# Attention gates with their weights stationary in four column groups, and the empty bank jobs moved to POOL

## The chip, the cores and the metric

The kernel runs on one core of one Trainium2 chip. The metric is the device time of one execution in microseconds, the median of several runs. All data are f32.

## The reference

Two transformer blocks in a row, over 256 tokens of 1024 channels, batch 1.

- The first block modulates the input by a projection of `c` (`ada_w`), projects it by `w_in`, and runs two branches: a gated linear recurrence over 8 heads (HGRN2: q, f, v, g) and a sparse attention over 8 heads (NSA: q, compressed, selected and window keys and values). Both are merged under gates, projected (`w_out`), and followed by a mixture of 32 experts with two chosen per token.
- The second block has cross attention on `mem`, a convolution, a bidirectional RWKV recurrence and 16 experts that choose their tokens.

What the change touches is one line of the attention:

```
gate = sigmoid(h @ w_in[:, 6656:6680] + b_in[6656:6680])     # 24 = 8 heads x 3 kinds
o = gate[..., 0:1] * o_c + gate[..., 1:2] * o_s + gate[..., 2:3] * o_w
```

`h` is 256 tokens x 1024 channels, so the product has only 24 columns.

## The kernel before

Each engine has its own instruction stream, written out in order; they meet only at semaphores.

**Weights.** SP loads weight tiles of up to 128 x 4096 f32 (2 MB) into a ring of 6 slots, in the order of the list `w`. Tile n is issued once the last job that reads tile n - 6 is full (`tile_read`, `last_job`). Biases go to a small area of rows (`brow`). POOL issues the small loads and the scattered ones.

**Banks.** The output memory of TensorE has 8 banks of 128 x 512. Every group of products is a job with a number that `PLAN1` and `PLAN2` give in order; job j uses bank j mod 8. `start(j)` makes TensorE wait until job j - 8, the one before in the bank, has been copied out. `fills` raises the bank's "full" semaphore, `frees` its "free" one; `is_full` and `is_out` wait for them. So two counters for each bank replace a list of dependencies, and a job that isn't needed must still raise both. The plan has 6 such empty jobs, `unused`, between the attention and the branch products `br`. TensorE raises all twelve counts itself, just ahead of `br`.

**Products.** `mm` is one product, recorded at L1447 for nearly all of them. An f32 product shows in the trace as two matmul records and two weight loads. `hT` is the modulated input, channels on partitions, 8 chunks (k) of 128 channels x 256 tokens. `chunk_pair` gives outputs with channels on partitions: a 128x128 piece of weights is stationary, 256 tokens move. `token_half` gives outputs with tokens on partitions: 128 tokens of `hT` are stationary, the weights' columns move. Where 4 products with 32 stationary columns each are given to the four column groups (`32 * q:32 * q + 32`), they run side by side and leave four partial sums, which a product with a selection matrix such as `fold` adds up (`modulation`, the compression's `part` and `hid`).

**The order around the change, on TensorE.** q, f, v, g, nq, kvc, ks, vs, kw, vw; then the gates: for each of two token halves a bias row and 8 products of 24 moving columns (`token_half`, L1447); then `part` (2 jobs of 32 products, from the compression's weights `cw1`), `hid` (their folding), `kcmp`, `vcmp`; then the recurrence (KT, att, and per head updates, outputs and half of a merge gate), `turn_heads` 0 to 2, and the attention by heads: `scores(0)`, and for each head h `scores(h + 1)`, modulation products (`ada2`) and `weigh(h)`. For h = 0 `turn_heads(3)`, which waits for the last two normalised heads of DVE, comes before the products of merge gate 2.

**On ScalarE (ACT).** It copies out most jobs, in the same order. Around the gates: `ks`, `kw`; L1035 Sigmoid of the gates; L1040 the two `part` copies; L1043 Silu of `hid`; L1046 and L1048 `kcmp`, `vcmp`. A function of another table set needs an ACT_TABLE_LOAD just ahead of it: Exp at L1031, then Sigmoid, then Silu.

**On POOL.** It waits for `rel` to be copied out, writes the rows of relative biases to DRAM (`relrow`, 2 MB), waits for that, and then for the values `v` and `vs`, and for the gates to be full (their bias row lies where it writes), and masks the values for the recurrence.

Of the kernel before, what the change touches and what calls it, by code (L numbers as in the profile page):

```python
# [53 lines left out]
def constants():  # L54
    t = np.arange(P)
    same = (t[:, None] // CHUNK) == (t[None, :] // CHUNK)
    return pack({
        "ident": np.eye(P),
        "upto": same & (t[:, None] <= t[None, :]),
        "scan": np.tile((np.arange(T) % CHUNK != 0), (P, 1)),  # L60
        "seen": (t[:, None] + P * np.arange(TT)[None, :]) >= 31,
        "odd": t[:, None] // CHUNK % 2 == np.arange(2)[None, :],
        "mhalf": np.full((P, 1), -0.5),
        "eps_conv": np.full((P, 1), 1e-5),
        "eps_group": np.full((P, 1), 64e-5),
        "fold": (t[:, None] % 32 == np.arange(30)[None, :]),
        "gkey": np.tile(4 - np.arange(4), (P, 1)),
        "ekey": np.tile(NE1 - np.arange(NE1), (P, 1)),
        "pick": (t[:, None] % CHUNK == np.arange(CHUNK)[None, :]),
        "fold16": (np.where(t // 32 % 2 == 0, t % 32, t % 32 - 16)[:, None] == np.arange(16)[None, :]),  # L70
        "until": t[:, None] <= t[None, :],
        "fold36": (np.where(t < 64, t, t - 92)[:, None] == np.arange(36)[None, :]),
    })
# [19 lines left out]
def scan_masks():  # L93
# [5 lines left out]
    for d, late in enumerate((i < j, i > j)):  # L99
        parts[f"strictT{d}"] = late  # L100
        parts[f"uptoT{d}"] = late | (i == j)
        for m in MERGES:
# [4 lines left out]
CST, CST_A = constants()  # L107
MSK, MSK_A = scan_masks()
UP0 = 4
PAGED = (4, 5, 12, 13)  # L110

VA = dict(b=0, mg=52, l0=68, l1=76, hgn=84, nmix=92, nmem=100, nffn=108)
# [1 line left out]
VROWS = (116, 62, 93, 64)  # L114
N_VEC = 23

PLAN1 = [("mod", 1), ("hT", 2), ("modc", 1), ("q", 4), ("hTb", 2), ("modb", 1), ("modcb", 1), ("rel", 3), ("f", 4), ("v", 4), ("g", 4), ("nq", 4),
         ("kvc", 2), ("ks", 1), ("vs", 2), ("kw", 1), ("vw", 2), ("gate", 1), ("part", 2), ("hid", 2), ("kcmp", 1), ("vcmp", 1),
         ("KT", 4), ("att", 4), ("hg", 3 * HEADS + 4), ("OHT", 3),
         ("nsa", 6 * HEADS + 15), ("unused", 6), ("br", 8),  # L120
         ("g1b", 2), ("y", 4), ("memT", 4), ("h2T", 4), ("modc2", 1), ("vm", 1),
         ("logitT", 1), ("route", 1), ("gain", 1), ("km", 1), ("rank1", 1), ("general", 19)]
IN2 = (2, 3, 4, 0, 1)
# [10 lines left out]
def build(nc, A, out):  # L134
    with ExitStack() as ctx:
# [141 lines left out]
        def last_job(n):  # L277

            name, i = w[n][0], [m for m in range(N2) if w[m][0] == w[n][0]].index(n)
            if name == "mg":  # L280
                return jM0(3) if i == 0 else jG(2 * i + 1)
            if name == "ada":
                return J(("mod", "modb")[i // 2]) if i < 4 else jA(i - 4)
            if name == "in2":
                return (J("in2", 1), J("in2", 3), J("in2", 5), J("qa"), J("in2b", 1))[i]
            if name in ("gate", "cw1"):
                return J({"gate": "gate", "cw1": "part"}[name], i)
            if name in ("q", "f", "v", "g", "nq", "kvc", "br", "wout2"):
                return J({"wout2": "y2"}.get(name, name), 2 * i + 1)
            if name == "wout":  # L290
                return J("y", 2 + i)
            return J(*{"kvs": ("vs", 1), "kvw": ("vw", 1), "cw2": ("vcmp", 0), "mem": ("km", 0), "router": ("logitT", 0),
                       "up2": ("a1", 1), "router2": ("scoreT", 0)}[name])
# [28 lines left out]
        VV = v4(vv[:], TT, 2)  # L322
        blocks = [arena(7)[:, 0:962], arena(7)[:, 1024:1986]]
        hpart = v3(arena(9)[:, 384:640], 2)
        h1 = v3(arena(9)[:, 0:60], 2)
        kcmp = arena(9)[:, 64:94]
        vcmp = v3(arena(9)[0:NBLK, 128:384], 2)
# [75 lines left out]
        for h in range(HEADS):  # L403
            if h + 1 < HEADS:
                nsa += [("scores", h + 1, i) for i in range(3)]
            if h == 0:
                nsa += [("turn", 3, 0), ("gate", 2, 0)]
            nsa += [("ada", i, 0) for i in ADA_BEFORE[h]]
            nsa += [("out", h, i) for i in range(2)]
            if 0 < h < HEADS - 2:  # L410
                nsa.append(("gate", h + 2, 0))
            nsa += [("ada", i, 0) for i in ADA_WITHIN[h]]
            nsa.append(("out", h, 2))
# [334 lines left out]
        def _(pool):  # L748
# [48 lines left out]
            load(relrow, relsb.unsqueeze(1).to_broadcast([HEADS, P, 2 * T]), "rel_stored")  # L797
            pool.wait_ge(S("rel_stored"), 16)

            def bias_rows(dst, h0, count, name):  # L800

                for t in range(TT):
                    src = bass.AP(relrow.tensor, 255 - P * t + P * 2 * T * h0,
                                  [[2 * T - 1, P], [P * 2 * T, count], [1, T]])
                    load(dst[:, :, t * T:t * T + T], src, name)
# [157 lines left out]
        def _(act):  # L963
# [67 lines left out]
            nc.scalar.activation(L[:], B[:], ACT.Exp).then_inc(S("forget_out"), 1)  # L1031
            chunks("ks", 0, ks, ACT.Identity, 44)
            chunks("kw", 0, kw, ACT.Identity, 48)
            is_full(act, J("gate"))
            frees(nc.scalar.activation(gates, v3(bank(J("gate"), 48), TT), ACT.Sigmoid), J("gate"))  # L1035
            for i in range(2):
                is_full(act, J("part", i))
                if i == 0:
                    is_full(act, J("part", 1))
                frees(nc.scalar.copy(hpart[:, i, :], bank(J("part", i), P)), J("part", i))  # L1040
            for i in range(2):
                is_full(act, J("hid", i))
                frees(nc.scalar.activation(h1[:, i, :], bank(J("hid", i), 30), ACT.Silu, bias=col(1, VB["b1k"] + i)),  # L1043
# [68 lines left out]
            exps(0)  # L1112
            for h in range(HEADS):
                if h == 0:
                    heads_turned(3)
                    gate_pair(2)
                carry_turned(h)
                if h + 1 < HEADS:
                    exps(h + 1)
# [296 lines left out]
        def _(pe):  # L1416
# [164 lines left out]
            for name in ("v", "g"):  # L1581
                for i in range(2):
                    n = tile(name)
                    for t in range(TT):
                        ins, j = token_half(name, 2 * i + t, slot(n, (8, 512)), 0, 512, hT, t)
                        fills(ins, j)
            for i in range(2):
                n = tile("nq")
                for c in range(2):
# [4 lines left out]
            for s in "sw":  # L1594
                n = tile("kv" + s)
                chunk_pair("k" + s, 0, slot(n, (8, 512)), 0, hT)
                for t in range(TT):
                    ins, j = token_half("v" + s, t, slot(n, (8, 512)), 256, 256, hT, t)
                    fills(ins, j)
            n = tile("gate")  # L1600
            j = job("gate")
            for t in range(TT):
                ins, _ = token_half("gate", 0, slot(n, (8, 24)), 0, 24, hT, t, brow_at(n)[1][:, 0:24],
                                    bank(j)[:, 24 * t:24 * t + 24], j)
            fills(ins, j)

            for i in range(2):
# [4 lines left out]
                for p in range(32):  # L1612
                    q = p % 4
                    ins = mm(bank(j, P)[32 * q:32 * q + 32, :], blocks[i][:, 30 * p:30 * p + 32],
                             slot(n, (32, 128))[:, p, :], p < 4, p >= 28)
                fills(ins, j)
            for i in range(2):
                is_out(pe, J("part", i))
                j = job("hid", i)
# [152 lines left out]
            for h in range(HEADS):  # L1772
# [1 line left out]
                    scores(h + 1)  # L1774

                if h == 0:
                    turn_heads(3)
                    n_mg.append(tile("mg"))
                    products(start(jG(2)), slot(n_mg[0], (8, 512)), 0, hT)
                for i in ADA_BEFORE[h]:  # L1780
                    pe.wait_ge(S("slide_ready"), 2)
                    ada2(i)
# [2 lines left out]
            for j in range(4):  # L1785
                is_out(pe, jOHT(j))
            is_out(pe, jT(HEADS - 1, 2))
            for i in range(6):
                j = job("unused", i)
                pe.sem_inc(full[j % BANKS], 1)  # L1790
                pe.sem_inc(free[j % BANKS], 1)  # L1791
            for i in range(4):
                n = tile("br")
                for c in range(2):
# [1644 lines left out]
```

## Time and profile before

| | us |
|---|---|
| median of 3 runs | 1648.62 |
| lowest and highest | 1647.56, 1656.34 |
| the profiled execution, its own time | 1652.61 |
| its span (first to last instruction) | 1650.4 |
| PE busy | 1346.3 (82%) |
| DVE busy | 425.1 (26%) |
| ACT busy | 278.7 (17%) |
| POOL busy | 124.7 (8%) |

PE is TensorE, PEld its weight loads, which run beside the products. The granted clock is a share of 2.4 GHz: 1.00 is 2.4 GHz and 0.50 is 1.2 GHz. Its mean over the span is 0.901. A DMA share of 1 means that all 16 DMA engines are busy. The times in the views are counted from the start of the span.

### The profile page before, as it was taken

How to read it: one execution, taken by the hardware profiler on the slowest of the kernel's cores; microseconds unless marked ns; L12 is line 12 of the kernel's file. 1: busy time of each engine (PE TensorE's matmuls, PEld its weight loads, DVE VectorE, ACT ScalarE, POOL GpSimd, SP SyncE). 2: the span in 40 equal slices, each digit the busy share in tenths (PEclk: the TensorE clock that was granted, in tenths of full speed). 3: DMA queues.
4: the chain of work that ended last, by engine and by line, in shares of the span. 5: the costliest groups of instructions: out<-in, count | busy, mean ns of one | idle time of the engine just before them, and what ended most of it. 6: DMA issues, size and time to landing. Idle time of an engine off the chain costs nothing.

```text
span 1650.4 us, 27106 instructions
## 1 busy us (share of the span) xinstructions
PE 1346.3 (82%) x11720; PEld 757.5 (46%) x11720; DVE 425.1 (26%) x910; ACT 278.7 (17%) x626; POOL 124.7 (8%) x283
## 2 busy tenths in 40 slices
PE   5999999999999877777777689877887576766675
PEld 4756887777663332322322278676432122212221
DVE  1012147430273222222222234563520000000001
ACT  0201224550011111110111113332110100100000
POOL 4000013000000000000000004021000000000000
PEclk9999999999999998988998989987888778787778
DMA  9865383566469999999999690300989999999996
GB/s 347 266 175 210 106 296 120 186 222 207 156 261 425 426 428 427 429 428 428 428 429 427 285 340 29 95 4 8 414 326 428 428 429 428 428 428 428 428 427 272
DMA packets 86997, 513.90 MB, mean 311 GB/s; under 512 B 9033, under 2 KB 13562, under 8 KB 62338
## 3 DMA queue, kind: packets, MB, share of 16 engines
q1 hardware_dynamic: 82306, 502.84, 75.1%
q0 software_dynamic: 3936, 9.19, 2.3%
q8 instruction: 66, 1.08, 0.3%
q10 hardware_dynamic: 672, 0.65, 0.2%
q14 instruction: 17, 0.14, 0.0%
HBM read 507.77 MB, written 3.15 MB: 310 GB/s over the span
## 4 chain that ended last, share of the span: by engine, by line
PE 50%; DMA 41%; DVE 4%; issue 2%; ACT 1%; SPq 1%; POOL 0%; DVEq 0%; PEldq 0%; ACTq 0%
PE ps L1447 41%; DMA ring<-in_exp_w 19%; DMA arena<-in_w_e_down 19%; PE ps L2241 4%; DMA ring<-in_w_e_up 2%; PE ps L1536 2%; DMA ring<-in_w_in 1%; DVE stats L2600 1%; PE ps L2013 1%; DMA arena<-in_mem 1%; PE ps L2441 0%; PE ps L1491 0%; PE ps L1676 0%; SPq L636 0%; PE ps L1672 0%
## 5 line engine op out<-in xcount | busy, mean ns | idle before, releaser
L1447 PE MATMUL ps<-ring,arena 128*32 128x512 f32 (+4 forms) x1844 | 264.4, 646 | 105.5 <-DMA ring<-in_exp_w 89.1
L1447 PE MATMUL ps<-ring,hTs 128*32 128x512 f32 (+3 forms) x1056 | 232.4, 624 | 33.9 <-DMA ring<-in_w_e_up 21.3
L1447 PE MATMUL ps<-hTs,ring 128*128 128x256 f32 (+2 forms) x992 | 216.3, 385 | 0.1
L1447 PEld LDWEIGHTS ps<-ring,arena 128*32 128x32 f32 (+1 forms) x1844 | 84.8, 128 | 265.1 <-issue 241.5
L1447 PEld LDWEIGHTS ps<-hTs,ring 128*128 128x128 f32 (+2 forms) x992 | 183.6, 189 | 29.0 <-issue 4.2
L1447 PE MATMUL ps<-arena,vv 128*32 128x512 f32 (+2 forms) x560 | 98.2, 756 | 86.3 <-DMA arena<-in_w_e_down 81.9
L1447 PEld LDWEIGHTS ps<-ring,hTs 128*32 128x32 f32 (+1 forms) x1056 | 88.1, 141 | 152.2 <-issue 114.1
L1447 PEld LDWEIGHTS ps<-arena,vv 128*32 128x32 f32 (+2 forms) x560 | 28.8, 148 | 139.4 <-DMA arena<-in_w_e_down 88.5
L1447 PE MATMUL ps<-arena,hTs 128*32 128x512 f32 x480 | 92.5, 621 | 0.0
L3001 DVE COPY hTs<-ps 64x512 f32<-64x512 f32 x32 | 22.2, 693 | 259.7 <-PE ps L1447 259.7
L1177 ACT COPY arena<-ps 128x512 f32<-128x512 f32 x32 | 18.7, 585 | 388.4 <-PE ps L1991 388.4
L1447 PE MATMUL ps<-arena,ring 128*128 128x256 f32 (+2 forms) x320 | 71.2, 388 | 3.8 <-PEq L1791 2.6
L1447 PEld LDWEIGHTS ps<-arena,ring 128*128 128x128 f32 (+1 forms) x320 | 60.0, 193 | 14.8 <-issue 6.7
L2013 PE MATMUL ps<-arena 64*128 64x512 f32 x256 | 63.0, 610 | 1.6 <-DVE arena L3010 1.6
L3381 DVE TENSOR_TENSOR vv<-vv,ps 64x512 f32<-64x512 f32 x16 | 11.0, 690 | 204.7 <-ACT vv L1396 204.7
L3375 DVE TENSOR_TENSOR hTs<-ps,nffn 128x128 f32<-128x128 f32 x32 | 7.8, 286 | 204.5 <-PE ps L1447 204.5
L857 POOL COPY arena<-arena 128x128 f32 (+1 forms) x64 | 16.9, 293 | 437.9 <-PE ps L1991 417.3
L1447 PEld LDWEIGHTS ps<-cst,low 64*128 64x128 f32 (+1 forms) x544 | 33.1, 189 | 27.4 <-issue 27.4
L1396 ACT ACTIVATE vv<-ps 64x512 f32<-64x512 f32 x16 | 9.4, 590 | 201.1 <-PE ps L1447 201.1
L1447 PE MATMUL ps<-arena 128*32 128x512 f32 (+6 forms) x264 | 43.3, 411 | 0.0
L2529 PE MATMUL ps<-hTs,vv 64*128 64x512 f32 x128 | 38.2, 724 | 1.4 <-ACT hTs L1402 1.4
L1402 ACT COPY hTs<-ps 128x512 f32<-128x512 f32 x16 | 9.4, 585 | 172.9 <-PE ps L1447 172.9
(464 smaller groups left out, 1432.2 us busy)
## 6 DMA issues: line engine op xcount, KB each, us to landing
ring<-in_exp_w SPq DMA_DIRECT2D x92, 2048.0 KB, 22.2
arena<-in_w_e_down SPq DMA_DIRECT2D x28, 2048.0 KB, 25.6
ring<-in_w_e_gate SPq DMA_DIRECT2D x24, 2048.0 KB, 30.9
ring<-in_w_e_up SPq DMA_DIRECT2D x24, 2048.0 KB, 36.3
ring<-in_w_in SPq DMA_DIRECT2D x22, 2048.0 KB, 19.5
ring<-in_ada_w SPq DMA_DIRECT2D x12, 2048.0 KB, 17.2
arena<-in_w_e_up SPq DMA_DIRECT2D x8, 2048.0 KB, 34.6
arena<-in_w_e_gate SPq DMA_DIRECT2D x8, 2048.0 KB, 32.7
```

Source lines behind the costliest of these rows:

```text
L857: ins = nc.gpsimd.tensor_copy(gateR[:, t], mid(gatep1[:, t, cols], 4))
L1177: nc.scalar.copy(HT1, ps[:, m * 512:m * 512 + 512]).then_inc(S("hidT1_ready"), 1)
L1396: nc.scalar.activation(hid2, u[0:64], ACT.Silu).then_inc(S("silu2_ready"), 1)
L1402: nc.scalar.copy(YE, ps[:, 1024:1536]).then_inc(S("ye_ready"), 1)
L1447: return nc.tensor.matmul(o, lhsT, rhs, start=start, stop=stop)
L1536: ins = nc.tensor.matmul(o, wt[:, k, c * P:(c + 1) * P], hT[:, k, :], start=k == 0 and c % 2 == 0, stop=k == KC - 1, skip_group_check=True)
L2013: ins = nc.tensor.matmul(ps[:, b * 512:b * 512 + 512], HT1[r, 256 + t * P:256 + (t + 1) * P], YE1[r, :], start=False, stop=True, skip_grou ...
L2241: return nc.tensor.matmul(o, lhsT, rhs, start=start, stop=True, skip_group_check=True)
L2529: ins = nc.tensor.matmul(ps[:, b * 512:b * 512 + 512], HT2[r, 256 + t * P:256 + (t + 1) * P], YE[r, :], start=False, stop=True, skip_group ...
L2600: ins = nc.vector.bn_stats(bns[:, t, c, :], src[:, t, c * 512:(c + 1) * 512])
L3001: cp(part1, u[64:128]).then_inc(S("part_ready"), 1)
L3381: tt(hid2, hid2, ps[64:128, (e % 2) * 512:(e % 2) * 512 + 512], ALU.mult).then_inc(S("hid2_ready"), 1)
```

## The change

The gates are computed with the weights stationary. A chunk of 128 channels has 24 columns of gate weights; 32 are taken, so that a chunk brings some of its neighbour's. Chunk k goes to column group k mod 4, and 256 tokens move, 8 products in all, in a new job `gateT`. ACT copies its 128 x 256 result to the arena, and after `part` TensorE adds the four groups by a product of that copy with the selection matrix `fold24`, together with the bias row, in the job `gate`. ACT's Sigmoid now comes after the two `part` copies. The slot of the gates' weights is given back with `gateT`.

The empty jobs are 5 in place of 6, come before `nq`, and are raised by POOL after `relrow` is written, each once the job before it in its bank is out. For head 0, `turn_heads(3)` and the products of merge gate 2 change places, on TensorE, in the plan and on ACT.

```diff
+        "fold24": np.where(t < 96, t % 32, t - 104)[:, None] == np.arange(24)[None, :],
+UNUSED = 5
-... ("g", 4), ("nq", 4),
-         ("kvc", 2), ("ks", 1), ("vs", 2), ("kw", 1), ("vw", 2), ("gate", 1), ("part", 2), ("hid", 2), ...
+... ("g", 4), ("unused", UNUSED), ("nq", 4),
+         ("kvc", 2), ("ks", 1), ("vs", 2), ("kw", 1), ("vw", 2), ("gateT", 1), ("part", 2), ("gate", 1), ("hid", 2), ...
-         ("nsa", 6 * HEADS + 15), ("unused", 6), ("br", 8),
+         ("nsa", 6 * HEADS + 15), ("br", 8),
+        gateT = arena(9)[:, 640:896]
-                nsa += [("turn", 3, 0), ("gate", 2, 0)]
+                nsa += [("gate", 2, 0), ("turn", 3, 0)]
 # POOL, after relrow is stored
+            for i in range(UNUSED):
+                j = J("unused", i)
+                pool.wait_ge(free[j % BANKS], j // BANKS)
+                pool.sem_inc(full[j % BANKS], 1)
+                pool.sem_inc(free[j % BANKS], 1)
 # ACT
-            is_full(act, J("gate"))
-            frees(nc.scalar.activation(gates, v3(bank(J("gate"), 48), TT), ACT.Sigmoid), J("gate"))
+            is_full(act, J("gateT"))
+            act.wait_ge(S("blocks_ready"), 2)
+            frees(nc.scalar.copy(gateT, bank(J("gateT"), T)), J("gateT"))
             for i in range(2):
                 ... # the two part copies
+            is_full(act, J("gate"))
+            frees(nc.scalar.activation(gates, v3(bank(J("gate"), 48), TT), ACT.Sigmoid), J("gate"))
...
+                    gate_pair(2)
                     heads_turned(3)
-                    gate_pair(2)
 # TensorE
+            turn[0] += UNUSED
-            n = tile("gate")
-            j = job("gate")
-            for t in range(TT):
-                ins, _ = token_half("gate", 0, slot(n, (8, 24)), 0, 24, hT, t, brow_at(n)[1][:, 0:24],
-                                    bank(j)[:, 24 * t:24 * t + 24], j)
+            n_gate = tile("gate")
+            j = job("gateT")
+            flat = slot(n_gate, (8, 24)).rearrange("p k n -> p (k n)")
+            for k in range(KC):
+                q = k % 4
+                o = 24 * k - 8 * (q // 3)
+                ins = mm(bank(j, T)[32 * q:32 * q + 32, :], flat[:, o:o + 32], hT[:, k, :], k < 4, k > 3)
             fills(ins, j)
             ... # the two part jobs
+            is_out(pe, J("gateT"))
+            j = job("gate")
+            for t in range(TT):
+                o = bank(j)[:, 24 * t:24 * t + 24]
+                mm(o, ones_row, brow_at(n_gate)[1][:, 0:24], True, False)
+                ins = mm(o, gateT[:, t * P:(t + 1) * P], C("fold24"), False, True)
+            fills(ins, j)
...
-                    turn_heads(3)
                     n_mg.append(tile("mg"))
                     products(start(jG(2)), slot(n_mg[0], (8, 512)), 0, hT)
+                    turn_heads(3)
...
-            for i in range(6):
-                j = job("unused", i)
-                pe.sem_inc(full[j % BANKS], 1)
-                pe.sem_inc(free[j % BANKS], 1)
```

## Rows read from the trace of the kernel before

**Rows 1.** The page, DMA rate in 40 equal slices of the span.

```profile
GB/s 347 266 175 210 106 296 120 186 222 207 156 261 425 426 428 427 429 428 428 428 429 427 285 340 29 95 4 8 414 326 428 428 429 428 428 428 428 428 427 272
```

**Rows 2.** Busy time by stage: length, PE, PEld, DVE, ACT, POOL, clock, DMA share, GB/s.

```profile
67.00:219.00 152.00, 151.94 (x578) 109.36 (x576) 26.06 (x38) 22.76 (x38) 1.10 (x1) 1.00 0.59 177
...
376.00:436.00 60.00, 57.50 (x258) 50.16 (x259) 7.17 (x11) 0.30 (x1) 1.61 (x3) 0.97 0.50 167
436.00:498.00 62.00, 60.33 (x294) 34.42 (x292) 38.84 (x88) 8.98 (x20) 4.75 (x9) 1.00 0.63 242
548.00:934.00 386.00, 296.90 (x2242) 113.66 (x2240) 94.32 (x158) 41.88 (x78) 19.38 (x79) 0.90 1.01 427
```

**Rows 3.** The chain that ended last: start, us, what.

```profile
189.82 40.72 PE ps L1447 x300
...
231.57 1.18 issue
...
437.43 9.57 DMA arena<-in_mem
```

**Rows 4.** Timeline at the gates: start, us, engine, line, operation, count, idle before.

```profile
225.11 5.38 PE L1447 MATMUL ps<-ring,arena 128*32 128x128 f32 x128
...
225.22 0.21 ACT L1035 ACTIVATE stats<-ps 128x48 f32<-128x48 f32 x1 [10.77 <-PE ps L1447]
...
231.07 1.28 ACT L1043 ACT_TABLE_LOAD   x1
232.37 0.46 ACT L1043 ACTIVATE arena<-ps,low 128x30 f32<-128x30 f32 x2
```

**Rows 5.** Busy time and granted clock in pieces of the gates' stretch.

```profile
219.10:219.43 0.33, 0.33 (x3) 0.29 (x2) 0.21 (x1) 0.00 (x0) 0.00 (x0) 1.00 0.00 0
219.43:221.40 1.97, 1.97 (x18) 1.93 (x17) 0.21 (x1) 0.00 (x0) 0.00 (x0) 1.00 0.53 108
221.65:225.10 3.45, 3.45 (x17) 3.40 (x16) 0.00 (x0) 0.00 (x0) 0.00 (x0) 0.52 1.05 404
225.10:228.30 3.20, 3.20 (x61) 2.96 (x64) 0.00 (x0) 0.21 (x1) 2.85 (x5) 0.50 0.94 281
228.70:230.50 1.80, 1.79 (x68) 1.52 (x56) 0.00 (x0) 0.00 (x0) 0.00 (x0) 1.00 1.03 397
```

**Rows 6.** Products in four column groups: a chain row (256 columns), a timeline row.

```profile
1040.90 10.57 PE ps L1447 x192
...
371.44 1.90 PE L1447 MATMUL ps<-ring,low 128*32 128x512 f32 x16
```

**Rows 7.** Timeline, 275 to 301 us: scores, heads, gate product, DVE's softmax.

```profile
275.10 3.68 PE L1447 MATMUL ps<-arena 128*128 128x15 f32 x24
...
280.58 0.66 PE L1696 MATMUL ps<-cst,arena 128*128 128x128 f32 x4 [1.80 <-DVE arena L2775]
...
281.08 7.07 PE L1447 MATMUL ps<-hTs,ring 128*128 128x256 f32 x32
...
299.44 1.28 DVE L2821 TENSOR_SCALAR arena<-arena,stats 128x15 f32<-128x15 f32 x6
```

**Rows 8.** Timeline and granted clock at the empty jobs.

```profile
375.93 0.37 ACT L1110 COPY arena<-ps 128x256 f32<-128x256 f32 x1 [5.46 <-PE ps L1447]
...
378.50 1.77 PE L1447 MATMUL ps<-arena,ring 128*128 128x256 f32 x4 [2.60 <-PEq L1791]
...
379.00:382.00 3.00, 3.00 (x8) 2.37 (x8) 0.00 (x0) 0.00 (x0) 0.00 (x0) 0.50 1.05 386
```

**Rows 9.** Evictions of `v` and `g`, and the write of `relrow`.

```profile
68.46 1.10 POOL L750 DMA_DIRECT2D relrow<-arena  x1 [40.30 <-ACT arena L1014]
...
102.18 0.69 DVE L2702 TENSOR_TENSOR arena<-ps,low 128x512 f32<-128x512 f32 x1 [3.32 <-PE ps L1447]
...
150.15 0.69 DVE L2702 TENSOR_TENSOR arena<-ps,low 128x512 f32<-128x512 f32 x1 [5.67 <-PE ps L1447]
...
relrow<-arena POOLq DMA_DIRECT2D x1, 2048.0 KB, 44.8
```

More of the change, by code:

```diff
@@ L115 @@
 N_VEC = 23
-PLAN1 = [("mod", 1), ("hT", 2), ("modc", 1), ("q", 4), ("hTb", 2), ("modb", 1), ("modcb", 1), ("rel", 3), ("f", 4), ("v", 4), ("g", 4), ("nq", 4),
-         ("kvc", 2), ("ks", 1), ("vs", 2), ("kw", 1), ("vw", 2), ("gate", 1), ("part", 2), ("hid", 2), ("kcmp", 1), ("vcmp", 1),
+PLAN1 = [("mod", 1), ("hT", 2), ("modc", 1), ("q", 4), ("hTb", 2), ("modb", 1), ("modcb", 1), ("rel", 3), ("f", 4), ("v", 4), ("g", 4), ("unused", UNUSED), ("nq", 4),
+         ("kvc", 2), ("ks", 1), ("vs", 2), ("kw", 1), ("vw", 2), ("gateT", 1), ("part", 2), ("gate", 1), ("hid", 2), ("kcmp", 1), ("vcmp", 1),
          ("KT", 4), ("att", 4), ("hg", 3 * HEADS + 4), ("OHT", 3),
-         ("nsa", 6 * HEADS + 15), ("unused", 6), ("br", 8),
+         ("nsa", 6 * HEADS + 15), ("br", 8),
          ("g1b", 2), ("y", 4), ("memT", 4), ("h2T", 4), ("modc2", 1), ("vm", 1),
@@ L286, in last_job @@
             if name in ("gate", "cw1"):
-                return J({"gate": "gate", "cw1": "part"}[name], i)
+                return J({"gate": "gateT", "cw1": "part"}[name], i)
             if name in ("q", "f", "v", "g", "nq", "kvc", "br", "wout2"):
```

## The prediction

> **What bounds the kernel now.** I began with the page's DMA slices: the rate lies at 4 to 350 GB/s in some of them and at 425 or more in the others [rows 1], so no one resource bounds the whole. The busy time by stage says which does where [rows 2]: from 67 to 219 us PE is busy 151.94 of 152.00 us; from 548 to 934 us the DMA share is 1.01 and PE is busy only 296.90 of 386. The edits lie in the first, PE-bound third. There, every microsecond in which PE works or waits is a microsecond of the span, if it also moves the start of the expert stream. It should: at 436 to 498 us the DMA share is 0.63 and in the 60 us before 0.50 [rows 2], so the stream is not yet full, and what its issues and the load of `mem` wait for are products and norms behind PE. The chain of waits agrees [rows 3]: an unbroken run of L1447 up to 230.5 us, an "issue" of 1.18 us that ends at 232.75, and much later the `mem` load at 437.43, which starts behind PE's last branch products. The gates, PE's wait for the normalised heads and its empty jobs all lie ahead of that load.
>
> **A. The gates (219.11 to 232.75 us).** Now: 16 products of 128x24 and two bias rows, 219.11 to 225.11, 6.00 us; then 128 records of the partial sums, 5.38 us; then ACT's two copies, a table load of 1.28 us, Silu, and PE goes on at 232.75 [rows 4]. Two records are one f32 product. The clock matters: it was 1.00 for the first eight gate products (1.97 us), then 0.52 for the second eight (3.45 us), 0.50 for the first part of the partial sums, and 1.00 again from 228.70, where 68 records took 1.80 us, 26 ns each [rows 5]. It fell from 2.4 to 1.2 GHz after 2.4 us of very narrow products.
>
> The new gateT product is 16 records of 128*32 stationary and 256 moving columns, in four column groups. The trace has the form: 192 such records took 10.57 us at clock 1.00, so 16 take 0.88; 16 records of twice the columns took 1.90, half of which is 0.95 [rows 6]. The outer bounds are 0.88 and, if the groups did not overlap, 16 x 0.22 us as in the full-width rows (32 records in 7.07 us, [rows 7]), 3.5 us. I take 0.96, the nearest rows. The partial sums then run behind wide products at full clock: 128 x 26 to 27.5 ns = 3.5 us (at worst 5.38 again). The fold job: two bias rows at 0.32 us (219.11 to 219.43) and two folds at 0.25 (1.97/8) = 1.14 us.
>
> On the new clock of this stretch: gateT ends at 220.07, the partial sums at 223.6, the fold at 224.75, and the `hid` products behind it at 225.4. ACT copies gateT (0.37 us, the 128x256 copy of [rows 8]) while PE is in the partial sums, so PE's new wait for it costs nothing; if that copy were late, the fold, `hid` and all of PE's queue would stand behind it. But the Sigmoid now stands between the copies and the Silu. Its table load of 1.28 us lay in time in which ACT had nothing to do (10.77 us idle before the Sigmoid, [rows 4]); now copies end at 224.1, Sigmoid's load at 225.4, Sigmoid (0.21) at 225.6, Silu's load at 226.9, and with 0.35 us from Silu's start to PE's, PE goes on at 227.3. Against 232.75 that is 5.4 us less. The moved load costs 1.5 us of what would be 6.9.
>
> From 223.6 to about 228.2 PE then has only narrow products (24, 30, 15 columns) and 1.9 us of nothing. In this trace 2.4 us of such work was followed by half clock, so I expect one fall here. Its price, from the fall of [rows 8]: 3.0 us at 0.50 and, as an estimate from it, 0.4 at its edges, half of which is lost, 1.7 us. Bounds: 0 and two such stretches, 3.4. A yields 3.7 us (2.0 to 5.4; with groups that do not overlap or slow partial sums down to 0).
>
> By the Trainium skill, ScalarE: Activation LUTs, "What ACT_TABLE_LOAD costs", a switch costs 1283 ns of load and about 1380 ns of drain. The load's length is that of the trace; the drain isn't seen (Silu starts 0.02 us after the load's end). With a drain counted as well for the moved load, A would be 2.3 instead of 3.7.
>
> **B. Gate product ahead of the last head turn (278.8 to 288.1 us).** PE ends the scores of head 1 at 278.78, waits 1.80 us for the normalised heads (DVE L2775), turns them in 0.66 and then does the 7.07 us gate product, whose inputs are long there [rows 7]. In the new order it runs in the gap: 278.8 to 285.9, then the turn, about 286.4 instead of 288.1. All 1.80 us are gained, since the modulation products that follow wait only for a DVE step ahead of those heads in its queue. What is late next: DVE's additions of masks to head rows that a load brings, and behind them the softmax of head 1, whose exps run on ACT behind the copies of head 0's turned weights and so move with PE; that DVE step ends at 300.72 [rows 7], 8 us after the additions have to be done. ACT's two evictions are swapped likewise; nothing waits on the turn before 376 us. Bounds 0 and 1.8.
>
> **C. The empty jobs.** PE stands idle 375.9 to 378.5, 2.60 us, for ACT's last copy (375.93 and 0.37 us) and then for its own twelve increments (its sequencer's L1791 is named as releaser) [rows 8]. Without them PE starts its products at about 376.6: 1.9 us. Behind this gap the clock is 0.50 from 379 to 382 [rows 8]; with a gap of 0.7 us I expect no fall, another 1.7 us (0 to 1.7, since the fall may not come in every execution). Together 3.6.
>
> By the Trainium skill, TensorE: Matmul & The Clock Gate, "A second HAM failure mode: psum-queue depth-cycling", frequent micro-idles between groups of products bring the clock down and up again. The trace agrees at 378.5 us; by that rule the new narrow stretch in A falls too, as counted, and a remaining 0.7 us gap in C could still do it, which would take C to 1.9.
>
> **D. Where the empty jobs go.** They now stand between `g` and `nq` and give banks a shift of 5 there. `nq` 0 to 2 wait for `g` 1 to 3 in place of `v` 0 to 2: the eight evictions of `v` and `g` run from 102.18 to 150.15, 6.9 us apart [rows 9], so each is over at least 6 us before its `nq` job, the first of which starts at 150. `nq` 3 comes at 150 + 3 x 6.9 = 170.7 and waits for POOL's first raise. POOL raises when the 2 MB write of `relrow` has landed (68.46 + 44.8 = 113.3) and, for the last, when `g` 0 is out (102.18 + 4 x 6.9 + 0.7 = 130.5) [rows 9]: 57 us of slack, nothing is paid, and what is queued behind the raises on POOL waits for the gates anyway. From the gates on all jobs keep their mutual distance. The 24 new constant columns are 12 KB, 0.04 us at the first slice's 347 GB/s. The tile loads released by gateT start 5 us earlier into a DMA whose share before 219 us is 0.59; nothing needs them before the modulation products of B. All this at 0; the bound is 0.3.
>
> **Sum.** 3.7 + 1.8 + 3.6 = 9.1 us. On the profiled execution: 1652.61 - 9.1 = 1643.5 (its span 1650.4 to 1641.3, with 2.2 us around it). The median of the runs is 1648.62, 4 us below it, so I forecast 1639.5.
>
> **The rivals.**
> 1. The clock stays up in A's narrow stretch (the trace shows no fall behind the partial sums, where `hid` and the products behind it were narrow too): 10.8 us, 1637.8.
> 2. The gates give less: half clock also over the partial sums (+1.9) or groups that don't overlap (+2.5), or two low stretches behind them (+1.7): 4.5 to 6.5 us gained, about 1643. For it: the partial sums ran at 0.50 in this trace. Against: what preceded them were 24-column products, which are gone.
> 3. Swallowed: the expert stream is DMA-bound and starts no earlier, 1648.6. For: DMA 1.01 from 548 us on. Against: 0.50 and 0.63 before, with issues that wait for PE. It would show as a longer DMA wait near 548 us. Smaller variants (other falls of the clock in later stages) give or take 2 to 4 us and end here too.
> 4. Slower: POOL raises too late. If `relrow` landed after 170.7 us instead of 113.3, PE would stand at `nq` 3, microsecond for microsecond; from 170.7 + 9.1 = 179.8 on the kernel is slower than before, at 190 us by 10 us: 1659. Only a write 66 us longer than the 44.8 seen would do it.
> 5. The change doesn't do what it says: DVE's heads come later than the gate product's end, or Sigmoid's load is put elsewhere. The second would help by 1.5 us.
>
> **Chances.** Forecast (1637.5 to 1641.5) 0.48; rival 1 0.12; rival 2 0.18; rival 3 0.16; rival 4 and anything slower 0.05; rival 5 0.01. The range reaches from rival 1 with 3 us below it to rival 3: 1634 to 1648. Half a per cent, about what a measurement of this kernel can tell from no change, is 8.2 us, or 1640.4. My forecast is just past it: faster by more 0.50 (two thirds of the forecast's share, rival 1, and some of rivals 2 and 5), within 0.45, slower 0.05.
>
> **What would show it.** Gates: one run of about 16 records in under 1.1 us at 219 us, partial sums in 3.5 us at clock 1.00, two table loads back to back before Silu, PE going on 8.2 us after the gates began. Heads: no wait for DVE L2775. Empty jobs: PE idle under 1 us before the branch products and 1.00 behind it. The `mem` load near 428 us. It is wrong if that load starts early and the end doesn't move, if the partial sums stay at 5 us, or if PE stands at `nq` 3.

## The result

The changed kernel takes 1639.33 us (median of 9 runs, 1636.01 to 1643.08). The kernel before, run beside it, takes 1650.31 us (9 runs, 1644.59 to 1656.83). The ratio is 0.9933, 95% interval 0.9914 to 0.9952. A later comparison (E11) gave 0.9954 [0.9939, 0.9969]. The forecast was 1639.5 us.

The profiled execution has a span of 1638.5 us, 11.9 less than the 1650.4 before. The chain of waits of the changed kernel (start, us, what), beside [rows 3]:

```profile
24.63 8.83 PE ps L1548 x32
...
189.79 34.32 PE ps L1459 x286
224.11 2.01 issue
226.12 0.92 PE ps L1459 x6
227.03 3.52 PE ps L1660 x16
...
369.64 84.75 PE ps L1459 x324
```

L1459 is what L1447 was. PE goes on at `kcmp` at 226.12 instead of 232.75, and its branch products start at 369.64 instead of 378.50 [rows 8]. The first row is a difference that isn't the change's: the same 32 records took 10.04 us in the trace of before. The clock was 0.50 from 24 to 30 us there and only from about 26 to 29 us here, and with a start 0.14 us earlier that gives 1.3 us.

The timeline of the changed kernel at the gates, which answers to [rows 4]:

```profile
217.77 1.07 PE L1459 MATMUL ps<-hTs,ring 128*32 128x256 f32 x16
...
218.66 3.68 PE L1459 MATMUL ps<-ring,arena 128*32 128x128 f32 x128
...
218.91 0.37 ACT L1045 COPY arena<-ps 128x256 f32<-128x256 f32 x1 [7.10 <-PE ps L1459]
...
222.46 0.43 ACT L1050 COPY arena<-ps 128x128 f32<-128x128 f32 x2 [3.17 <-PE ps L1459]
...
222.91 1.28 ACT L1052 ACT_TABLE_LOAD   x1
...
224.21 0.21 ACT L1052 ACTIVATE stats<-ps 128x48 f32<-128x48 f32 x1
224.43 1.28 ACT L1055 ACT_TABLE_LOAD   x1
225.73 0.46 ACT L1055 ACTIVATE arena<-ps,low 128x30 f32<-128x30 f32 x2
```

The gates' first product is 16 records that start 0.89 us before the partial sums; these run for 3.68 us, and two table loads with the Sigmoid between them stand ahead of Silu. The granted clock of the changed kernel there and behind it (length; busy PE, PEld, DVE, ACT, POOL; clock; DMA share; GB/s), beside [rows 5]:

```profile
219.00:222.00 3.00, 3.00 (x120) 3.00 (x114) 0.00 (x0) 0.29 (x1) 0.00 (x0) 1.00 0.95 309
223.00:226.00 3.00, 1.11 (x8) 0.96 (x8) 0.00 (x0) 2.96 (x5) 2.17 (x4) 1.00 1.05 394
227.00:230.00 3.00, 3.00 (x15) 3.00 (x15) 0.00 (x0) 1.83 (x6) 0.00 (x0) 0.50 1.05 385
230.50:233.00 2.50, 2.50 (x25) 2.50 (x24) 1.31 (x2) 0.65 (x2) 0.00 (x0) 1.00 1.01 373
```

The partial sums now run at 2.4 GHz. In the 3 us before 226 PE has 1.11 us of narrow products, and from 227 to 230 us, in the key turns, it is at 1.2 GHz: the fall that the forecast counted.

The swap and the gap ahead of the branch products in the timeline of the changed kernel, beside [rows 7, 8]; and the `mem` load, which started at 437.43 before:

```profile
270.09 3.68 PE L1459 MATMUL ps<-arena 128*128 128x15 f32 x24
273.61 7.07 PE L1459 MATMUL ps<-hTs,ring 128*128 128x256 f32 x32
280.52 0.60 PE L1718 MATMUL ps<-cst,arena 128*128 128x128 f32 x4
281.05 5.36 PE L1459 MATMUL ps<-ring,low 128*32 128x512 f32 x48
...
368.91 0.37 ACT L1122 COPY arena<-ps 128x256 f32<-128x256 f32 x1 [5.46 <-PE ps L1459]
...
369.64 1.53 PE L1459 MATMUL ps<-arena,ring 128*128 128x256 f32 x6 [0.77 <-ACT arena L1122]
...
426.88 0.71 POOL L753 DMA_DIRECT2D arena<-in_mem  x1 [48.18 <-DVE arena L2886]
```

No row of the first four has an idle time before it any more: the gate product starts 3.52 us after the scores, where the head turn started 5.48 us after them. The idle time ahead of the branch products is 0.77 us, released by ACT's last copy and not by PE's sequencer, and the clock stays at 1.00 behind it:

```profile
369.60:373.00 3.40, 3.36 (x16) 3.00 (x17) 0.00 (x0) 0.00 (x0) 0.00 (x0) 1.00 1.05 386
```

**Where the 11.9 us are, stage by stage in these two executions.** 1.3 us before 67 us, by the clock; 3.7 between the gates' start and the recurrence's first output (23.89 to 20.22); 2.0 at the swap; 1.8 in the gap ahead of the branch products and 1.7 in the 59 us behind it; 1.3 after the `mem` load. The stage from 66 to 219 us, into which the empty jobs went, is the same to 0.01 us.

### The profile page after: what moved, and what is told of

Same layout as the page of the kernel before. It is cut to its first block, busy times and chain, and to the rows that moved or that the text cites. A ratio compares the mean times of both kernels' runs of the same rounds, so it can differ in the third digit from the quotient of the medians.

```text
span 1638.5 us, 27083 instructions
## 1 busy us (share of the span) xinstructions
PE 1335.9 (82%) x11708; PEld 750.6 (46%) x11708; DVE 425.1 (26%) x910; ACT 279.5 (17%) x627; POOL 125.5 (8%) x283
## 4 chain that ended last, share of the span: by engine, by line
PE 52%; DMA 41%; DVE 3%; issue 2%; ACT 1%; SPq 1%; POOL 0%; DVEq 0%; ACTq 0%
PE ps L1459 42%; DMA arena<-in_w_e_down 19%; DMA ring<-in_exp_w 19%; PE ps L2259 4%; DMA ring<-in_w_e_up 2%; PE ps L1548 2%; DMA ring<-in_w_in 1%; PE ps L2031 1%; PE ps L1698 0%; SPq L639 0%; PE ps L1694 0%; DVE stats L2618 0%; PE ps L1503 0%; PE ps L2271 0%; PE ps L1759 0%
## 5 line engine op out<-in xcount | busy, mean ns | idle before, releaser
L1459 PE MATMUL ps<-ring,arena 128*32 128x512 f32 (+4 forms) x1844 | 263.9, 643 | 103.1 <-DMA ring<-in_exp_w 87.4
L1459 PE MATMUL ps<-ring,hTs 128*32 128x512 f32 (+2 forms) x1024 | 229.2, 641 | 42.1 <-DMA ring<-in_w_e_up 23.8
L1459 PE MATMUL ps<-hTs,ring 128*128 128x256 f32 (+2 forms) x1008 | 216.8, 384 | 0.1
L1459 PEld LDWEIGHTS ps<-ring,arena 128*32 128x32 f32 (+1 forms) x1844 | 83.6, 127 | 263.9 <-issue 241.7
L1459 PEld LDWEIGHTS ps<-hTs,ring 128*128 128x128 f32 (+2 forms) x1008 | 183.8, 188 | 29.4 <-issue 4.3
L1459 PE MATMUL ps<-arena,vv 128*32 128x512 f32 (+2 forms) x560 | 93.8, 722 | 85.3 <-DMA arena<-in_w_e_down 80.9
L1459 PEld LDWEIGHTS ps<-ring,hTs 128*32 128x32 f32 (+1 forms) x1024 | 82.9, 139 | 161.8 <-issue 115.3
L1459 PE MATMUL ps<-arena,hTs 128*32 128x512 f32 x480 | 93.9, 627 | 0.0
L1459 PEld LDWEIGHTS ps<-arena,vv 128*32 128x32 f32 (+2 forms) x560 | 28.3, 144 | 136.5 <-DMA arena<-in_w_e_down 87.4
L1459 PE MATMUL ps<-arena,ring 128*128 128x256 f32 (+2 forms) x320 | 69.5, 381 | 2.8 <-issue 2.0
L1459 PEld LDWEIGHTS ps<-arena,ring 128*128 128x128 f32 (+1 forms) x320 | 58.8, 190 | 13.3 <-issue 5.7
L1459 PEld LDWEIGHTS ps<-cst,low 64*128 64x128 f32 (+1 forms) x544 | 33.1, 189 | 27.4 <-issue 27.4
L1459 PE MATMUL ps<-arena 128*32 128x512 f32 (+6 forms) x264 | 43.3, 411 | 0.0
```

Of the source, the lines that this page charges most:

```text
L1459: return nc.tensor.matmul(o, lhsT, rhs, start=start, stop=stop)
```

## The experiments

Because the forecast came out so near, the question was whether its terms are right or only their sum. Each kernel's runs scatter by some 3 us (standard deviation), as much as a term is worth, so each experiment is read in two ways: by its timed ratio, and by the lengths of the stretches in its trace, which the later stages don't disturb. The table has the stretches that the change touches, from start times in the timelines, in us: from the gates' first product to `kcmp` (gates), on to the recurrence's first output (then), the two together (sum), from its last output group to the turn of head 0's weights (swap), from ACT's last copy to the branch products (gap), on to the `mem` load (branch), and from that load to the end (rest).

```
kernel                gates   then   sum    swap    gap   branch   rest     ratio [95%]
before                13.64  10.25  23.89   20.41   2.57   58.93  1212.97
E4  before again      13.67  11.81  25.48   20.41   2.54   58.70  1208.63
E2  empty jobs alone  10.40  10.25  20.65   20.40   0.74   57.24  1212.08   0.9993 [0.9972, 1.0014]
E3  swap alone        10.40  10.28  20.68   18.38   2.57   57.23  1212.89   0.9991 [0.9967, 1.0015]
E9  swap and empty    10.40  10.25  20.65   18.38   0.73   57.24  1217.25   0.9986 [0.9972, 1.0000]
E8  14 empty jobs     12.07  11.81  23.88   20.41   5.01   59.16  1209.41   1.0010 [0.9993, 1.0027]
E1  gates alone        8.34  12.74  21.08   20.41   2.27   58.92  1212.67   0.9998 [0.9978, 1.0019]
E10 gates and empty    8.34  11.87  20.21   20.40   0.73   57.24  1208.16   0.9955 [0.9940, 0.9970]
changed                8.35  11.87  20.22   18.38   0.73   57.24  1211.62   0.9933 [0.9914, 0.9952]
E11 changed again      8.34  12.71  21.05   18.39   0.73   57.24  1217.08   0.9954 [0.9939, 0.9969]
E7  one column group  10.92  12.77  23.69   18.38   0.73   57.24  1213.67   0.9963 [0.9945, 0.9981]
E5  fold late          6.81  11.82  18.63   18.39   0.73   57.23  1216.11   0.9935 [0.9913, 0.9957]
E6  key turns early    8.57   8.56  17.13   18.38   0.73   57.24  1213.31   0.9929 [0.9905, 0.9954]
E12 the same again     8.58   8.55  17.13   18.38   0.73   57.24  1209.06   0.9927 [0.9909, 0.9945]
```

**E1, the gates' part alone.** The changed kernel with the swap undone and its 5 empty jobs back on TensorE.

> The kernel before with the gates' part of the change alone (column groups, fold, Sigmoid behind the part copies; 5 empty jobs stay on TensorE ahead of the branch products, head turn stays first). Theory (three separate gains, gates 3.7, swap 1.8 to 2.0, empty jobs 3.5): 3 to 4 us faster, from the gates' start to the product after Silu 8.3 us in place of 13.6, one fall of the clock behind it, idle before DVE's heads 1.8 us and 2.2 us before the branch products as before. Rival (the gain of the whole is mostly luck with the clock in other places): this kernel within 1 us of before.

Measured: the gates' stretch is 8.34 us, as forecast, and the half clock behind it came and cost 2.5 us (12.74 for the 10.25 of the traces in which no fall came there). The timed ratio, 0.9998, shows nothing, with an interval that reaches to 3.6 us faster. By the trace the theory's path is right, but the whole stretch, 21.08 us, is then only 2.8 us shorter than in the first trace of before. By the time neither the theory nor the rival is decided.

**E2, the empty jobs alone.** The 6 empty jobs stand ahead of `nq` and POOL raises them.

```diff
-         ("nsa", 6 * HEADS + 15), ("unused", 6), ("br", 8),
+... ("g", 4), ("unused", 6), ("nq", 4), ...        # raised by POOL after relrow is stored
```

> The kernel before with the 6 empty jobs ahead of nq, raised by POOL, and nothing else changed. Theory: PE idle before the branch products 0.7 us in place of 2.6, granted clock 1.00 behind it in place of 0.50 for 3 us: 3.5 us faster (1.9 if before's clock does not fall in most executions). Rival: the fall at that place comes from something else than the gap and stays: 1.9 us or less. Second rival: POOL's raises make PE wait at the fourth nq job: a gap near 170 us; I expect none.

Measured: gap 0.74 us, and 57.24 us behind it, the length without a fall; no wait at the fourth `nq` job. By time it is 1.2 us faster with an interval from 4.6 faster to 2.3 slower, which decides nothing. The surprise was elsewhere. This kernel has the old gates, and in its timeline the second eight gate products take as long as the first, at full clock (timeline, then clock):

```profile
218.89 1.97 PE L1453 MATMUL ps<-ring,hTs 128*128 128x24 f32 x16
...
221.11 1.97 PE L1453 MATMUL ps<-ring,hTs 128*128 128x24 f32 x16
223.01 3.70 PE L1453 MATMUL ps<-ring,arena 128*32 128x128 f32 x128
```

```profile
218.50:220.50 2.00, 2.00 (x18) 1.90 (x17) 0.42 (x1) 0.00 (x0) 0.00 (x0) 1.00 0.34 62
220.50:222.20 1.70, 1.70 (x16) 1.63 (x15) 0.00 (x0) 0.00 (x0) 0.00 (x0) 1.00 0.97 354
```

The fall of the clock that [rows 5] show for the same instructions did not come: 4.4 us of 24-column products passed at 2.4 GHz.

**E3, the swap alone.**

> The kernel before with the products of merge gate 2 ahead of the last head turn and nothing else changed. Theory: the 1.80 us wait for DVE's heads is gone and no other wait takes its place: 1.8 to 2.0 us from the scores' end to the modulation products. Rival: the softmax of head 1 becomes the next wait and takes it back: PE idle over 0.3 us before its turned weights.

Measured: the stretch is 2.03 us shorter (18.38 for 20.41), the same in all eight traces with the swap but for 0.01 us, and 82.57 us follow it, up to ACT's last copy, in place of 82.56: nothing there takes it back. Of the 0.2 us above the wait of 1.80 [rows 7], 0.16 are the end of the scores: their last record ends 3.68 us after the first starts, and the gate product starts beside it, at 3.52. By time the kernel is 1.5 us faster, from 5.4 faster to 2.5 slower. The gap ahead of the branch products is there (2.57), but this time no fall behind it (the clock's windows of this kernel):

```profile
369.80:372.00 2.20, 0.02 (x1) 0.05 (x1) 0.00 (x0) 0.00 (x0) 0.00 (x0) 1.00 1.05 386
372.00:375.00 3.00, 3.00 (x14) 2.67 (x15) 0.00 (x0) 0.00 (x0) 0.00 (x0) 1.00 1.05 388
```

**E4, the kernel before, again.**

> The kernel before, unchanged, once more with a trace. Question: do the two falls of the clock (at the 24-column gate products, and behind the gap at the empty jobs) come in every execution? Theory: at the gates always, behind the gap of 2.6 us perhaps in this one, perhaps not; the rest of the stages agrees within 0.1 us, apart from where the clock falls or rises.

Measured: both falls came, and a third between them. The clock fell inside the second eight gate products, was back at 1.00 for the wait behind the partial sums, and fell again in the narrow products behind it and the key turns (windows):

```profile
224.10:229.00 4.90, 4.90 (x95) 4.52 (x98) 0.00 (x0) 0.21 (x1) 2.85 (x5) 0.50 1.04 387
229.60:232.40 2.80, 1.25 (x28) 0.87 (x20) 0.00 (x0) 2.02 (x5) 0.00 (x0) 1.00 1.05 387
232.80:235.20 2.40, 2.40 (x12) 1.79 (x12) 0.00 (x0) 0.66 (x3) 0.00 (x0) 0.50 1.05 387
```

The first cost 3.3 us (13.67 for 10.40), the second 1.6 (11.81 for 10.25): 25.48 us in place of 23.89. With E2, E3, E8 and E9 there are six traces of the old gates: three with falls (23.89, 25.48, 23.88) and three without (20.65, 20.68, 20.65). In E8 the clock fell only in the partial sums, and once more behind the wait (see there). "At the gates always" was wrong.

**E5, the fold of the gates behind `hid`, the Sigmoid behind the `vcmp` copy.**

```diff
-... ("part", 2), ("gate", 1), ("hid", 2), ...
+... ("part", 2), ("hid", 2), ("gate", 1), ...      # and the Sigmoid behind the copy of vcmp
```

> The changed kernel, with the fold of the gates behind the hid products (in the time in which TensorE waits for Silu) and the gates' Sigmoid behind the vcmp copy. Theory (the moved Sigmoid, its table load and the fold lie on the path, 1.5 us of load and Sigmoid, 1.1 us of fold): PE goes on at kcmp 1.5 to 1.6 us earlier than in the changed kernel, 6.7 us after the gates begin in place of 8.35; the clock may still fall behind it. Rival: the Sigmoid was hidden (no drain and load beside others' work) and nothing is gained; or the KT copies on ACT, now behind one more table load, make PE wait before the first updates and take it back.

Measured: 6.81 us to `kcmp` in place of 8.34, the 1.5 us that the Sigmoid and its load cost. `kcmp` starts 0.38 us behind Silu, as in the changed kernel (0.39), so the path still runs over ACT, and the fold fits into the wait for Silu. The fall of the clock stays, 1.6 us, although PE has no wait left there, only narrow products. Timed, 0.9935 against before; that doesn't separate it from the changed kernel.

**E6, key turns directly behind `hid` as well.** On ACT the copies of the turned keys (KT) come ahead of those of `kcmp` and `vcmp`, and the Sigmoid behind all of them. The lines are set against E5.

```diff
-... ("hid", 2), ("gate", 1), ("kcmp", 1), ("vcmp", 1), ("KT", 4), ...
+... ("hid", 2), ("KT", 4), ("gate", 1), ("kcmp", 1), ("vcmp", 1), ...
```

> As the run before it, and the recurrence's key turns (KT, wide 128-column products) directly behind the hid products, then the fold, kcmp, vcmp. Theory (the clock falls because PE has only narrow products and a gap for over 2.4 us): the wide products stand in that stretch, no fall, PE never waits for Silu: from the gates' start to the end of att some 3.2 us less than in the changed kernel (1.6 of path and 1.7 of clock). Rival (the clock falls for another reason, or whatever is done there): only 1.6 us.

Measured: 17.13 us from the gates to the recurrence, 3.1 less than in the changed kernel, and no fall of the clock. Against E5, which had no wait there either and fell, the difference is the wide products in that place. Its ratio alone, 0.9929, was too near the changed kernel's; it was run again as E12.

**E7, one column group.**

```diff
-                q = k % 4
-                o = 24 * k - 8 * (q // 3)
-                ins = mm(bank(j, T)[32 * q:32 * q + 32, :], flat[:, o:o + 32], hT[:, k, :], k < 4, k > 3)
+                o = 24 * k
+                ins = mm(bank(j, T)[0:24, :], flat[:, o:o + 24], hT[:, k, :], k == 0, k == KC - 1)
...                                                    # copy and fold with 24 rows in place of 128
```

> The changed kernel with all 8 gate products in one column group (24 stationary columns each, one sum), the fold with 24 rows. Theory: the 16 records of 256 columns no longer overlap, 16 x 0.22 = 3.4 us in place of 1.07 us: 2.4 us slower. Rival (column groups give nothing for f32, the gain came from the wide moving side alone): no difference.

Measured: PE's partial sums start 3.04 us after the gates in place of 0.89, but the last gate record stands among them, and the fold starts 7.06 us after the gates in place of 4.50, so 2.56 us more (timeline):

```profile
219.25 3.42 PE L1459 MATMUL ps<-hTs,ring 128*24 128x256 f32 x15
222.29 0.42 PE L1459 MATMUL ps<-ring,arena 128*32 128x128 f32 x6
222.50 0.38 PE L1459 MATMUL ps<-hTs,ring 128*24 128x256 f32 x1
222.72 3.66 PE L1459 MATMUL ps<-ring,arena 128*32 128x128 f32 x122
226.31 0.40 PE L1459 MATMUL ps<-low,cst 1*128 1x24 f32 x2
```

The groups do overlap with f32 data, and the stretch up to `kcmp` says the same as the fold: 10.92 us for 8.34. So the groups are worth 2.6 us, near the 2.4 expected and more than the 2.06 by which the new stretch is shorter than the old one at full clock (8.34 for 10.40). With one column group the new form loses 0.5 us against it.

**E8, 14 empty jobs on TensorE.**

> The kernel before with 14 empty jobs raised by TensorE in place of 6 (28 increments in place of 12, same banks otherwise). Theory (each pair of increments costs PE 0.3 us on the path): the gap before the branch products is 2.6 + 8 x 0.3 = 5.0 us, and the clock falls behind it in every execution: 2.4 to 4 us slower than before. Rival: the gap is mostly a wait for the last copy and stays near 2.6.

Measured: the gap is 5.01 us for 28 increments and 2.57 for 12 (and 2.27 for the 10 of E1), so 0.15 us for each increment and 0.74 us of waiting for the copy. The fall came, partly inside the gap (clock window, then timeline):

```profile
374.70:379.60 4.90, 0.00 (x0) 0.00 (x1) 0.00 (x0) 0.29 (x1) 0.00 (x0) 0.70 1.05 387
```

```profile
379.63 2.90 PE L1447 MATMUL ps<-arena,ring 128*128 128x256 f32 x6 [5.05 <-PEq L1791]
```

By time it is 1.0010, from 1.2 us faster to 4.5 slower; the trace has 2.4 us more on the path, and the fall.

At the old gates, the 24-column products kept 2.4 GHz and the clock fell in the partial sums behind them (windows):

```profile
218.00:222.20 4.20, 4.20 (x36) 4.10 (x35) 0.34 (x1) 0.00 (x0) 0.00 (x0) 1.00 0.75 247
223.50:226.00 2.50, 2.50 (x56) 2.50 (x52) 0.00 (x0) 0.00 (x0) 1.85 (x4) 0.50 1.05 381
```

That cost 1.7 us (12.07 for 10.40), and the next fall, behind the wait, 1.6 (11.81 for 10.25).

**E9, swap and empty jobs together.**

> The kernel before with the swap and the moved empty jobs, the gates as before. In the traces the swap took 2.03 us and the empty jobs 1.84 us and mostly a fall of the clock (1.7 us) from the stretch up to the load of mem, each time; in timed runs neither alone stood clear of before. Theory (the gains are additive and reach the end; the single kernels' runs scatter by more than their gain): 3.9 to 5.6 us faster than before. Rival (the later, DMA-bound stages take back a gain of a few microseconds, and only a larger one comes through): within 2 us of before.

Measured: 0.9986 [0.9972, 1.0000], so 2.3 us faster, 0 to 4.6. That lies below the theory's 3.9 to 5.6 and just above the rival's 2, and the interval admits both. The load of `mem` starts at 427.75 us, 9.7 us before that of before, of which 3.2 are the old gates without their fall and 1 the first stage. Its rest, 1217.25, is 4.3 us longer than before's. Where, by the windows from the recurrence's end to the last block's experts, of the kernel before (first) and of this one:

```profile
1144.50:1196.00 51.50, 44.19 (x298) 25.89 (x290) 22.75 (x34) 10.89 (x21) 1.11 (x2) 0.86 0.81 334
```

```profile
1136.00:1191.40 55.40, 48.84 (x303) 29.53 (x293) 22.79 (x34) 10.90 (x21) 1.11 (x2) 0.78 0.78 317
```

The same instructions with a mean clock of 0.78 for 0.86 take 3.9 us more. DVE and ACT are busy for the same time (22.79 and 10.90 us for 22.75 and 10.89).

**E10, gates and empty jobs, no swap.**

> The changed kernel with the head turn first again (no swap). Theory, additive: the whole less 2.03 us, so 7 to 9 us faster than before; mem's load 2.0 us later than in the changed kernel. Rival (later stages take back small gains): somewhere between 0 and 3 us faster.

Measured: 0.9955, 7.4 us faster (5.0 to 9.9), in the range of the additive theory and outside that of its rival. The load of `mem` starts at 429.04 us, 2.2 later than in the changed kernel.

**E11, the changed kernel again.**

> The changed kernel, unchanged, once more with a trace and beside the two partial ones on one chip. Theory: mem's load at 427 us give or take 2 (the clock's fall behind the gates can come or not, and the start varies by 1.3), the whole 9 to 11 us faster than before. Rival (the 11 us of the first comparison were partly chance): 6 to 8 us.

Measured: `mem` at 428.62, within the forecast, and 0.9954, 7.6 us faster (5.1 to 10.1), which is the rival's 6 to 8 and not the theory's 9 to 11. The 11 us of the first comparison were partly chance, as far as one repetition tells: the rest was 1211.62 in its trace, here 1217.08. The two ratios together are about 0.994, some 9 us.

E9, E10 and E11 ran beside the same runs of before, so their ratios also give single parts. The gates (E11 against E9) are worth 5.3 us by time, with some 3.4 of uncertainty. The swap (E11 against E10) is worth 0.2 us, with some 3.5, where each trace with the swap has 2.0: that gain isn't shown in time.

**E12, E6 again, on the chip of E9 to E11.**

> The kernel with the key turns directly behind hid and the fold behind them, once more, now on the chip of the changed kernel. By the trace of its first run the gates' stretch is 3.1 us shorter than in the changed kernel. Theory (additive): 2 to 3.5 us faster than the changed kernel, 12 to 14 faster than before. Rival (nothing of it reaches the end): equal to the changed kernel.

Measured: 1637.64 us median against 1642.93 of the changed kernel beside it, ratios 0.9927 and 0.9954 against the same runs of before, so 4.5 us faster than it by the ratios where 2 to 3.5 were expected. The stretch is 17.13 us again, at full clock throughout (windows, then timeline):

```profile
223.00:226.00 3.00, 2.56 (x42) 2.29 (x31) 0.00 (x0) 2.26 (x6) 0.00 (x0) 1.00 1.03 398
226.00:229.00 3.00, 3.00 (x23) 2.45 (x21) 0.00 (x0) 2.63 (x11) 1.07 (x2) 1.00 1.05 386
```

```profile
224.03 0.63 PE L1459 MATMUL ps<-cst,arena 128*128 128x30 f32 x4 [0.44 <-ACT arena L1050]
...
224.49 1.95 PE L1641 MATMUL ps<-cst,arena 128*128 128x128 f32 x16
225.46 0.46 ACT L1053 ACTIVATE arena<-ps,low 128x30 f32<-128x30 f32 x2
...
227.60 0.39 PE L1459 MATMUL ps<-arena,ring 128*128 128x30 f32 x2
```

PE turns the keys and folds the gates while ACT loads Silu's table, and meets no wait at `kcmp`. With E6 it is the fastest kernel of this study: 12 us faster than before (9.1 to 15.0). That it beats the changed kernel as well is shown in the trace (3.9 us in this stretch against E11, 3.1 against the first trace) and likely in time (4.5 us by the ratios, whose intervals overlap a little: 0.9909 to 0.9945 and 0.9939 to 0.9969).

## Why the prediction was right, point by point

- **The bound.** Right: what PE saved ahead of 437 us moved the `mem` load by as much (10.55 us), and the end came 11.9 us earlier.
- **A, the path.** gateT 0.96 forecast, 0.89 measured; partial sums 3.5, 3.6 to the fold's start; PE at `kcmp` 8.2 us after the gates' start, measured 8.35. The cost of the moved Sigmoid, 1.5 us, is what E5 gained.
- **A, the fall behind it.** 1.7 forecast. It came in all six traces in which the new gates are followed by narrow products alone, and cost 1.6 to 2.5 us. It came in neither of the two in which the wide key turns stand there. Of rival 1, the clock staying up, there was no case, although behind the old gates the clock did stay up there in four of six traces. Why the new order always lost it isn't shown.
- **A, the size.** 3.7 forecast, 3.67 between the two first traces, and yet mis-sized as an average: the forecast took before's fall at the old gates for granted. That fall is 3.2 of the 5.4 us that it counted for the path (13.64 for 10.40 without it), and falls came there in three of six executions. At one and the same clock the path is 2.06 us shorter, and the fall behind the new gates takes as much back: the old stretch without a fall (20.65) is as long as the changed one (20.21 to 21.08). The mean of six old ones is 22.5 us, of the changed stretch (four traces) 20.6: 1.9 us, with an uncertainty of as much, since six executions are few. The weak step is the sentence that the clock "fell from 2.4 to 1.2 GHz after 2.4 us of very narrow products", taken for something that happens each time.
- **B.** 1.80 forecast, 2.03 measured in eight traces, nothing behind it late. By time it isn't shown (E3, and E11 against E10).
- **C.** 1.9 of idle forecast, 1.84 measured. The fall behind the gap, 1.7 forecast, is 1.69 and came in four of five traces with the gap and in none of the nine without: 1.3 us as an average. The caution in the forecast ("may not come in every execution") was in place. Its other one, that a remaining gap of 0.7 us could still bring a fall, was not borne out. The row at 378.5 us, which it set beside frequent micro-idles, shows one idle time of 2.60 us and not frequent ones.
- **D.** 0 forecast, 0.01 measured. POOL's raises were long done.
- **The sum.** 9.1 forecast. The traces' averages give 1.90 + 2.03 + 1.84 + 1.35 = 7.1, the two timed comparisons 11.0 and 7.6. So the forecast time was met to 0.2 us partly by luck: the terms of one execution, in which both of before's falls happened to be present, against a comparison in which the rest of the program ran well for the changed kernel.
- **Rival 2.** Its sum doesn't come out: 9.1 less 1.9, 2.5 or 1.7 is 6.6 to 7.4 us, and about 5 takes two of its items at once. None of them came: partial sums at full clock (3.61 us), groups that overlap, one low stretch.
- **Rival 3, swallowed.** Not as forecast: the 478 us that begin 37 us after the `mem` load, in which the expert stream lies, start 10.55 us earlier and take 477.90 us where they took 478.48. But its smaller variants, other falls of the clock, are what hides single terms: the rest after the `mem` load varies from 1208.2 to 1217.3 us over 14 traces in which nothing in it was changed. Its mean is 1212.2 with the old gates (six traces) and 1212.7 with the new ones (eight).

**What stays open.** The three parts alone gave 0.3, 1.2 and 1.5 us in timed runs, each with some 3.4 us of uncertainty, together 3 where the traces up to `mem` say 7 and the whole gave 8 to 11. The intervals admit this as chance. Harder to square is E10: gates and empty jobs together gave 7.4 us, alone 0.3 and 1.2, and the 5.9 between them are at the edge of what the three intervals allow (some 5.5). Whether the later stages systematically return part of a small gain isn't settled. So the whole is shown by time, and of the parts the gates beside the other two (5.3 us, E11 against E9), which is more than the 1.9 us of the traces' averages but admits them; the swap and the empty jobs are shown by their stretches of the trace alone.

By the Trainium skill, ScalarE: Activation LUTs, "What ACT_TABLE_LOAD costs", a switch has a drain of about 1380 ns beside its 1283 ns of load. The changed kernel's two switches in a row show 1.28 us each and their activations 0.02 us behind, so no drain here; the forecast was right to leave it out.

By the Trainium skill, TensorE: Matmul & The Clock Gate, "What's actually happening", the place of a change of clock varies from run to run of one kernel. The six traces of the old gates agree (20.65 to 25.48 us), and the forecast should have weighed before's fall by this.

## What to carry to other kernels

A product with few output columns belongs on the stationary side in column groups, with a selection product behind it; but look where its fold and its eviction then land, since here a table load on the path returned 1.5 of the 3.6 us that the form gives at full clock (10.40 us for 6.81 in E5). Increments that keep counters in step cost 0.15 us each on TensorE where it bounds the time, and nothing on POOL, which had time. And fill a wait of TensorE with wide products that are ready (key turns here): in both traces of that order the wait was gone, and the fall of the clock behind it too.

## What the runs showed of the hardware

The fall to 1.2 GHz comes in some executions of one and the same stretch and not in others. The 24-column products over 4.4 us kept 2.4 GHz in four executions (E2, E3, E8, E9) and lost it in two (before, E4); in E8 it went in the partial sums behind them. A gap of 2.3 to 5.0 us went with half clock in or behind it in four of five, one of 0.73 us in none of nine. One fall cost 1.5 to 3.3 us where PE is the bound. A difference of two single traces therefore carries several microseconds of such luck (1.8 us before 67 us, up to 5 at the old gates, up to 9 after the `mem` load), and a term is only as good as the number of executions that it was seen in.
